# Holding the last four weight units tile by tile, and opening each stage with four units on two token tiles

## What is computed

```
for l in range(DEPTH):
    x = layer_norm(ALPHA * x + 0.5 * swiglu(x, ffn1_w_gu[l], ffn1_w_down[l]), ln1_g[l], ln1_b[l])
    x = layer_norm(ALPHA * x + hybrid_mixer(x, w_in[l], ..., w_out[l]), ln2_g[l], ln2_b[l])
    x = layer_norm(ALPHA * x + 0.5 * swiglu(x, ffn2_w_gu[l], ffn2_w_down[l]), ln3_g[l], ln3_b[l])
```

## Time and profile before

| | us |
|---|---|
| median of 3 runs | 3951.83 |
| lowest and highest run | 3950.11 and 3959.24 |
| the profiled execution, its own time | 3947.34 |
| its span, first to last instruction | 3945.5 |
| TensorE busy | 3518.7 (89% of the span) |
| VectorE busy | 1716.8 (44%) |
| ScalarE busy | 1093.7 (28%) |
| mean granted TensorE clock | 0.93 of full |

### The profile page before, as it was taken

One profiled execution on the slowest core, in us unless ns is written; L12 is line 12 of the kernel. 1 busy time (PEld: TensorE's weight loads), 2 busy tenths in 40 slices (PEclk: granted clock), 3 DMA queues, 4 the chain that ended last, 5 costly groups with the idle time before them and its releaser, 6 DMA issues.

```text
span 3945.5 us, 42056 instructions
## 1 busy us (share of the span) xinstructions
PE 3518.7 (89%) x16608; PEld 2820.3 (71%) x16608; DVE 1716.8 (44%) x2388; ACT 1093.7 (28%) x1605; POOL 180.4 (5%) x254
## 2 busy tenths in 40 slices
PE   7888999978988889887999878899989997888998
PEld 4776667856766668866888755788878886667886
DVE  4445643325444653335333474433243326644333
ACT  3223422213312432212332224233123212333321
POOL 0010000000000000000000010000000002000000
PEclk9999998978999899978999987999999998889999
DMA  6222121022312110032223210222322321112231
GB/s 206 75 70 69 64 77 58 28 81 89 126 64 71 62 59 22 12 101 65 102 97 102 88 48 26 79 99 97 107 75 97 107 96 57 49 54 85 97 107 70
DMA packets 84740, 309.38 MB, mean 78 GB/s; under 512 B 9824, under 2 KB 10208, under 8 KB 84032
## 3 DMA queue, kind: packets, MB, share of 16 engines
q1 hardware_dynamic: 78192, 282.70, 21.3%
q0 software_dynamic: 6352, 24.00, 1.7%
HBM read 301.94 MB, written 4.72 MB: 78 GB/s over the span
## 4 chain that ended last, share of the span: by engine, by line
PE 53%; DVE 10%; ACT 3%; POOL 1%; issue 1%; DMA 0%; DVEq 0%; ACTq 0%; POOLq 0%; SPq 0%
PE bank L496 16%; PE bank L497 15%; PE bank L498 15%; PE bank L767 2%; DVE acc L1004 2%; PE bank L502 1%; DVE xn L1004 1%; DVE wlo L998 1%; PE bank L982 1%; DVE hl L998 1%; ACT pr L1695 1%; POOL stat L2164 1%; DVE G L998 0%; DMA raw<-in_W 0%; DVE stat L1536 0%
## 5 line engine op out<-in xcount | busy, mean ns | idle before, releaser
L496 PE MATMUL bank<-hh,whi 128*128 128x512 f32 (+1 forms) x2720 | 1099.3, 404 | 131.7 <-DVE wlo L998 65.5
L497 PE MATMUL bank<-hl,whi 128*128 128x512 f32 (+1 forms) x2720 | 1063.6, 391 | 0.0
L498 PE MATMUL bank<-hh,wlo 128*128 128x512 f32 (+1 forms) x2720 | 1063.0, 391 | 0.0
L998 DVE TENSOR_TENSOR wlo<-raw,whi 128x1024 fp32r<-128x1024 f32 x482 | 591.2, 1227 | 870.7 <-ACT whi L1700 841.1
L1700 ACT CAST whi<-raw 128x1024 fp32r<-128x1024 f32 x482 | 506.1, 1050 | 943.8 <-PE bank L498 813.6
L496 PEld LDWEIGHTS bank<-hh,whi 128*128 128x128 f32 x2720 | 530.9, 195 | 269.2 <-issue 139.7
L498 PEld LDWEIGHTS bank<-hh,wlo 128*128 128x128 f32 x2720 | 528.6, 194 | 105.1
L497 PEld LDWEIGHTS bank<-hl,whi 128*128 128x128 f32 x2720 | 530.7, 195 | 96.2 <-issue 4.8
L497 PE MATMUL bank<-wlo,fh 128*128 128x512 f32 x704 | 280.9, 399 | 0.0
L496 PE MATMUL bank<-whi,fh 128*128 128x512 f32 x704 | 277.6, 394 | 0.0
L498 PE MATMUL bank<-whi,fl 128*128 128x512 f32 x704 | 276.0, 392 | 0.0
(11 more groups left out here) (303 smaller groups left out, 3751.3 us busy)
## 6 DMA issues: line engine op xcount, KB each, us to landing
raw<-in_W SPq DMA_DIRECT2D x530, 512.0 KB, 3.3
bc<-in_ln_g POOLq DMA_DIRECT2D x6, 512.0 KB, 4.1
bc<-in_ln_b POOLq DMA_DIRECT2D x6, 512.0 KB, 5.6
xn<-in_x SPq DMA_DIRECT2D x4, 512.0 KB, 8.7
invcnt<-in_invcnt POOLq DMA_DIRECT2D x2, 1024.0 KB, 5.8
decay<-in_decay POOLq DMA_DIRECT2D x2, 1024.0 KB, 8.4
xn<-in_x POOLq DMA_DIRECT2D x4, 512.0 KB, 6.0
xd<-xn POOLq DMA_DIRECT2D x4, 512.0 KB, 2.9
```

Of the source, the lines that this page charges most:

```text
L496: e.matmul(out, ah, bh, start=first, stop=False, skip_group_check=True)
L497: e.matmul(out, ah, bl, start=False, stop=False, skip_group_check=True)
L498: return e.matmul(out, al, bh, start=False, stop=last, skip_group_check=True)
L998: return self.e.tensor_tensor(o, a, b, op)
```

## The change

Three edits. In the second half of `project`, `late` becomes 4: four units are held and run tile by tile. TensorE signals `used` for each held unit when its part of tile 3 is done, and the transposes of tile 0 stand after the second held unit of tile 2, those of tile 1 after the first held unit of tile 3. In `halves`, four units run over tiles 0 and 1, with the transposes of tile 2 after the second and those of tile 3 after the fourth, and then the four units run over tiles 2 and 3. All four banks are asked for before the first matmul. On ACT and DVE the taking of units moves accordingly, and DVE's layer norm is cut into `centre` and `scale`, with a `turn` or a weight unit between them.

```diff
@@ TensorE.halves
         for key, c in zip(keys, cols):
-            wh, wl, i = self.unit(name, index, t_pieces(c))
-            jobs.append((key, wh, wl, i, self.bank(self.all4, key)))
+            jobs.append((key,) + self.coming(name, index, t_pieces(c)) + (self.bank(self.all4, key),))
         for hf in range(2):
-            if hf:
-                self.to_hT_tile(st, 2)
-                self.to_hT_tile(st, 3)
-            for key, wh, wl, i, bank in jobs:
-                self.wait_ge(("hh", st, 2 * hf + 1, 1), ("hl", st, 2 * hf + 1, 1))
+            for n, (key, wh, wl, i, bank) in enumerate(jobs):
+                self.wait_ge(("hi", i), ("lo", i), ("hh", st, 2 * hf + 1, 1), ("hl", st, 2 * hf + 1, 1))
...
                 if hf:
                     t.then_inc(*self.up(key, ("used", i)))
+                elif n in (1, 3):
+                    self.to_hT_tile(st, 2 + n // 2)
@@ TensorE.tiles
-                if q == len(order) - 1:
-                    spent = [("used", h[3]) for h in held]
-                    a.then_inc(*(self.up(keys[t], *spent) if k == nk - 1 else self.up(*spent)))
-                elif k == nk - 1:
-                    a.then_inc(*self.up(keys[t]))
+                done = [keys[t]] if k == nk - 1 else []
+                if t == 3 and j:
+                    done.append(("used", i))
+                if done:
+                    a.then_inc(*self.up(*done))
+                if j and len(held) == late:
                     yield
@@ TensorE.project
-                                             (1, 2)[half])):
-                if half and t > 1 and nxt != ("ffn1", DEPTH):
-                    self.to_hT_tile(nxt, t - 2)
+                                             (1, 4)[half])):
+                if half and n in (9, 12) and nxt != ("ffn1", DEPTH):
+                    self.to_hT_tile(nxt, n // 12)
@@ VectorE.ffn and ScalarE.ffn
-            if m:
+            if m > 1:
                 self.now()
                 self.now()
@@ VectorE.project
             for t in range(4):
+                if half and t == 2 and nxt != ("ffn1", DEPTH):
+                    self.turn(nxt, 0)
                 if t == 3:
-                    for i in range(self.n_taken - late, self.n_taken):
-                        self.spend(i)
+                    self.spend(first + 1 if half else first)
+                    self.ahead()
...
                 if half:
+                    self.centre(st, t)
                     if t > 1 and nxt != ("ffn1", DEPTH):
-                        self.turn(nxt, t - 2)
-                    self.layer_norm(st, t, nxt)
+                        if t == 2:
+                            self.turn(nxt, 1)
+                        self.spend(first + 2 * t - 4)
+                        self.ahead()
+                    self.scale(st, t, nxt)
@@ ScalarE.project
+            first = self.n_taken - late
+            if half and nxt != ("ffn1", DEPTH):
+                self.turn(nxt, 0)
+            for i in range(first, first + (late + 1) // 2):
+                self.spend(i)
+            self.ahead()
+            if half and nxt != ("ffn1", DEPTH):
+                self.turn(nxt, 1)
+            for i in range(first, first + late):
+                self.spend(i)
```

More of the change, by code:

```diff
@@ L473, in bank, with coming @@
         return self.k.banks[slot]
-    def unit(self, name, index, pieces):
+    def coming(self, name, index, pieces):
         k = self.k
@@ L481, in unit @@
         k.split_of.append(i)
+        return k.halves(i) + (i,)
+    def unit(self, name, index, pieces):
+        wh, wl, i = self.coming(name, index, pieces)
         self.wait_ge(("hi", i), ("lo", i))
-        return k.halves(i) + (i,)
+        return wh, wl, i
     def direct(self, name, index, pieces):
@@ L870, in ffn @@
         self.at(st)
-        self.halves([("fg", st, 0), ("fu", st, 0)], name + "_w_gu_2", (l,), [0, FF], st)
-        for m in range(1, NFF):
+        self.halves([("fg", st, 0), ("fu", st, 0), ("fg", st, 1), ("fu", st, 1)], name + "_w_gu_2", (l,),
+                    [0, FF, 128, FF + 128], st)
+        for m in range(2, NFF):
             for key, col in (("fg", m * 128), ("fu", FF + m * 128)):
@@ L882, in project @@
             keys = [("pj", st, half, t) for t in range(4)]
-            for t, _ in enumerate(self.tiles(keys, name, (l,), k0s, 512 * half, xh, xl, ready, (self.ps, self.all4)[half],
-                                             (1, 2)[half])):
-                if half and t > 1 and nxt != ("ffn1", DEPTH):
-                    self.to_hT_tile(nxt, t - 2)
+            for n, _ in enumerate(self.tiles(keys, name, (l,), k0s, 512 * half, xh, xl, ready, (self.ps, self.all4)[half],
+                                             (1, 4)[half])):
+                if half and n in (9, 12) and nxt != ("ffn1", DEPTH):
+                    self.to_hT_tile(nxt, n // 12)
     def proj2(self, key, l, col, rota):
@@ L894, in mixer @@
         self.at(st)
-        self.halves([("ca", l, 0), ("cgt", l, 0)], "w_in_2", (l,), [1536, 1792], st)
-        drain(self.proj2(("ca", l, 1), l, 1664, self.all4))
-        drain(self.proj2(("cgt", l, 1), l, 1920, self.all4))
+        self.halves([("ca", l, 0), ("cgt", l, 0), ("ca", l, 1), ("cgt", l, 1)], "w_in_2", (l,), [1536, 1792, 1664, 1920], st)
         wide = self.wide_conv(l)
@@ L1494, in halves @@
     def halves(self, st):
-        a, b = self.take(), self.take()
+        used = [self.take() for _ in range(4)]
         self.turn(st, 2)
         self.turn(st, 3)
-        self.spend(a)
-        self.spend(b)
+        for i in used:
+            self.spend(i)
     def ffn(self, l, name, ln, nxt, eps):
@@ L1520, in project @@
         for half in range(2):
-            first = self.n_taken
-            late = (1, 2)[half]
+            late = (1, 4)[half]
             for ui in range(n):
@@ L1537, in project, with centre @@
                 if half:
+                    self.centre(st, t)
                     if t > 1 and nxt != ("ffn1", DEPTH):
-                        self.turn(nxt, t - 2)
-                    self.layer_norm(st, t, nxt)
-    def layer_norm(self, st, t, nxt):
+                        if t == 2:
[5 more added lines that the diff above has]
+                self.spend(i)
+    def centre(self, st, t):
         k = self.k
@@ L1548, in layer_norm, with scale @@
         self.stt(xt, xt, stat[:, 4 * t:4 * t + 1], k.bc[:, 0:1024], ALU.subtract, ALU.mult).then_inc(*self.up())
+    def scale(self, st, t, nxt):
+        k = self.k
+        stat, xt = k.stat, k.x_tile(t)
         self.wait_ge(("rows", st, 1), ("lnr", st, t))
```

7 lines of the change are left out of this document (removed).

## The result

The changed kernel took 3979.48 us (median of 4 runs, 3975.14 to 3987.68) against 3953.12 us for the kernel before in the same runs: a ratio of 1.0067, with a 95% interval from 1.0047 to 1.0088. It is slower by 26.4 us. The forecast was 3978 us, 25.9 above before.

The account below looks back on a forecast made before the run. TensorE's idles and lower clock were taken as the bound. Hand-overs +24.4, first feed-forward stage +4.8 and end -3.3 give +25.9 us: 3947.34 becomes 3973.2, plus 4.5 for the median, so 3978 us, range 3957 to 3992.

Parts of the forecast that it names:

- from the last matmul to the end: Program end, last unheld unit's last matmul to last scaling: 30.9 us in place of 34.8, so -3.9.
- What bounds: Whole kernel: only TensorE's idle or lower clock can be won; each hand-over loses 11.98 us idle and about 2.1 clock.
- Four held units: Hand-overs and last stage: idles ahead of transposes go, but the last held unit's slot brings a new idle of 2.75 us.
- The opening: Hand-over, first matmul of 256 columns: waits for the fourth bank, idle 5.2 us in place of 8.42.
- the chain of ten steps: Opening: ten steps in a row on three engines set TensorE's start at T = 29.4 after the first held matmul.
- The refill: Fifth unit N+4, behind pair 1 on ScalarE: new idle 4.2 us, 3.4 in a mixer.
- Shapes: Each stage: two more units run as matmuls of 256 columns in place of 512, costing 0.75 us.
- Clock: After idles: 2.1 us lost at the opening, 1.6 after idles of about 4 us, 0.6 after 2.75 us.
- the first idle: Ahead of the first held matmul: 2.75 us waiting for a weight's low half, with 0.6 us of clock taken.
- The faster case: Ring: halving of the last held unit and N+4 is covered, so 3926 us; chance 8%.
- The no-change case: New idles stand, but none is long enough to bring the clock down: about 3956 us; chance 14%.
- The slower one: Opening: VectorE loses another 3 to 4 us at each hand-over, about 3997 us; chance 9%.

Follow-up runs that it names:

- the kernel of 3895.5 us: Changed kernel with three held units, banks asked for one by one, N+4 split between the pairs, and tile 1's low half ahead of centring tile 2: 3895.52 us.
- the refill kernel: Changed kernel with ScalarE and VectorE splitting units N+4 and N+5 between the opening's two pairs again, not behind pair 1: 3940.39 us, ratio 0.997.

## Why the prediction was right

The mechanism was right wait by wait. The agreement of the total, 25.9 us forecast and 26.4 between the medians, is closer than the terms deserve. The two profiles differ by 33.2 us, because the profile before was of an execution 5.8 us below its median of 3953.12 and the one after 1.0 above its own. With the terms of the forecast sorted by kind (the idle of 2.75 us in the last stage among the idles), they stand against the profiles as follows, in us:

| | forecast | profiles |
|---|---|---|
| TensorE's idles in the second block | +13.8 | +13.9 |
| lower clock while it works there | +13.2 | +19.9 |
| shapes and restarts | +5.5 | +3.9 |
| from the last matmul to the end | -6.7 | -6.9 |
| first block and attentions | 0 | +2.3 |

So the idles were forecast to 0.1 us, and the clock was sized a third too low. That the medians don't show it is luck: their interval, 1.0047 to 1.0088, spans 19 to 35 us.

*What bounds.* Right: TensorE's idles and the clock after them make up nearly all of the change.

*Four held units.* Right in both directions. The transposes wait for nothing, and the new idle is 2.73 us in the feed-forward hand-overs and the last stage and 2.80 after the mixers (2.75 said). Three held units removed it.

*The opening.* Right, by the chain of ten steps: 5.27 us against 5.2, ended by the residual add (29.7 us after the first held matmul, 29.4 forecast). Asking for the banks one by one took it to 1.92, which shows that the bank and not `hl` or the weight was last.

*The refill.* Right: 4.17 and 3.3 us against 4.2 and 3.4. Splitting N+4 between the pairs removed this wait and no other. It was the dearest of the three: with four held units it is worth 39 us by the medians, 35 by the parts of the profiles that it touches. With two held, refill and banks mended together take 3992.0 to 3954.1 us, nearly all that the opening of four had cost by itself.

*Shapes.* The size holds. 96 matmuls of 256 columns took 11.6 us at the full clock (2936.32 to 2947.79 + 0.12), so the 48 of one unit take 5.80, where a unit at 512 columns takes 5.45: 0.7 us for the two units of a stage. The 0.1 us that the Trainium skill's figures gave ("TensorE: Matmul & The Clock Gate", "Back-to-back issue gap") does not hold here: these matmuls come at 0.121 us, where 262 cycles would be 0.109.

*Clock.* This is the term that was mis-sized: 13.2 us forecast, 19.9 in the profiles. I took 2.1 us for the opening, the same as before, 1.6 for the refill, 0.6 for the first idle, and nothing for 1.9 us. The profile after has 1.3 to 1.9 us at the opening, where that of before has 1.6 to 2.5; 1.6 to 2.3 at the refill; 1.6 after four of the six idles of 2.73 to 2.80 us and nothing after two; and 1.5 after four of the six idles of 1.9 us. The profile before had a case of it, 1.5 us after one of the five idles of 2.48, which I weighed for the first idle only. So the step that failed here is the one that took the shortest idle for harmless.

*The rivals.* The faster case asked for the two waits on ring slots to be covered, and the change did not meet this condition. No kernel here covers just these two. One covers the refill alone (39 us less) and one the last held unit alone (14 us less); if these added, it would be about 3926 us, an estimate, and that is the rival's figure. So its mechanism is borne out, though not shown by a kernel of its own. The argument against it, that such gaps stay whatever the order is, does not hold: the gap of 4.17 us went by an edit of the order alone, with the same ring of four. The no-change case fell with the clock, which did drop (its own sum gives 3954, not 3956: 3947.34 + 2.2 + 4.5). The slower one fell because the idle that ends VectorE's chain came out within 0.1 us.

## What to carry to other kernels

Holding units back to finish one tile early pays most while a free slot remains, one held unit fewer than the ring has: here four of four gained 10 us by themselves, and three of four another 14. Reordering one engine's stream moves what stands behind it too, as the memsets showed twice. When more units are put into an opening, look at what now stands behind the last of them in each helping engine's stream, and ask for an output bank when it is used, not earlier. The idles that a reordering leaves can be priced to a few tenths of a microsecond by adding up the last-arriving steps on each engine, in program order, from rows that exist; the clock behind them can't be priced so, and was most of what the forecast of the change and those of several edits missed.

## What the hardware did that I had not expected

An idle of 1.9 us can cost nearly as much clock as one of 4 us. In the changed kernel the same wait ahead of tiles 2 and 3, 1.90 or 1.91 us long in each stage, is followed by the level of 1.2 GHz in some stages and by the full 2.4 GHz in others. These are two stretches of 4 us right behind it, in the mixer and in the next feed-forward stage: length, busy times and counts, granted clock:

```profile
2263.20:2267.20 4.00, 3.98 (x21) 4.00 (x22) 0.00 (x0) 0.00 (x0) 0.00 (x0) 0.58 0.02 4
2550.50:2554.50 4.00, 3.99 (x33) 4.00 (x34) 0.00 (x0) 0.82 (x1) 0.00 (x0) 1.00 0.00 0
```

21 matmuls in the one, 33 in the other. It is all or nothing: about 1.5 us lost, in four of the six stages here. In the kernel with the refill mended it was two of six, after the same 1.91 us. TensorE had been at work for more than 10 us ahead of each. What decides between the two isn't shown by these runs.

The other thing is how much code that no edit touches moves. The first block is the same in all thirteen profiles and takes from 1844 us (the kernel of 3895.5 us) to 1854 us (three held units with the opening of two). In the former TensorE lost 109 us to the lower clock there, in the latter 123. The attention of the first mixer took 148.9 us in the profile before and in the one after, and 143.8 us in that of the refill kernel, with the same instructions there and 25, 24 and 17 us lost to the lower clock. So in these stretches the spread between executions goes with the clock. Differences of 5 to 10 us are why a gain of 2.4 us could be read from the idles only, and why a gain should be read from the part of the profile that the edit touches.
